# Half-piece runs, earlier table loads, reordered norm sums and unread products in a two-layer gated-mixer transformer kernel

## What is computed

```python
for l in range(DEPTH):
    ux = rmsnorm(h, g_pre_mix[l]) * (1 + sc1x) + sh1x
    yx, yc = token_mixers(ux, uc, ...)        # four attention branches A to D, gated, w_out
    h = h + ga1x * rmsnorm(yx, g_post_mix[l])
    ux = rmsnorm(h, g_pre_ffn[l]) * (1 + sc2x) + sh2x
    h = h + ga2x * rmsnorm(swiglu(ux, w_ffn_in[l], w_ffn_out[l]), g_post_ffn[l])
```

## Time and profile before

| | |
|---|---|
| median of 3 runs | 1987.03 us (1986.37 to 1988.64) |
| the profiled execution | 1986.53 us |
| its span, first to last instruction | 1984.1 us (2.4 us lie around it) |
| mean granted clock of TensorE | 0.962 of full speed |
| PE, DVE, ACT, POOL busy | 1832.9, 1218.5, 883.5, 679.9 us |

### The profile page before, as it was taken

One profiled execution on the slowest core, in us unless ns is written; L12 is line 12 of the kernel. 1 busy time (PEld: TensorE's weight loads), 2 busy tenths in 40 slices (PEclk: granted clock), 3 DMA queues, 4 the chain that ended last, 5 costly groups with the idle time before them and its releaser, 6 DMA issues. The chain is left out here.

```text
span 1984.1 us, 31794 instructions
## 1 busy us (share of the span) xinstructions
PE 1832.9 (92%) x10675; PEld 1584.5 (80%) x10675; DVE 1218.5 (61%) x2381; ACT 883.5 (45%) x1918; POOL 679.9 (34%) x615
## 2 busy tenths in 40 slices
PE   7888899999998999989999999788998889989998
PEld 7767778877877778778888878667887778879997
DVE  7345467776756865567677674655654446776654
ACT  2455544444433444452232333465554445555553
POOL 6143434445434544611111023134344444351100
PEclk9998999999998999979999999899999999989998
DMA  7221223333432323335456663123443333446663
GB/s 294 64 51 32 70 76 96 100 112 111 114 96 70 83 67 107 96 91 149 138 156 200 200 179 98 45 58 73 102 104 87 98 80 102 123 118 175 182 185 118
DMA packets 381802, 223.14 MB, mean 112 GB/s; under 512 B 51606, under 2 KB 377548, under 8 KB 380620
## 3 DMA queue, kind: packets, MB, share of 16 engines
q1 hardware_dynamic: 379340, 217.97, 38.8%
q10 hardware_dynamic: 2304, 3.15, 0.5%
HBM read 217.92 MB, written 3.15 MB: 111 GB/s over the span
## 5 line engine op out<-in xcount | busy, mean ns | idle before, releaser
L1808 PE MATMUL bank<-Uhi,w_ring 128*128 128x512 f32 (+2 forms) x1664 | 595.5, 358 | 27.9 <-DVE Ulo L1668 17.8
L1810 PE MATMUL bank<-Uhi,w_ring 128*128 128x512 f32 (+2 forms) x1664 | 580.5, 349 | 0.0
L1809 PE MATMUL bank<-Ulo,w_ring 128*128 128x512 f32 (+2 forms) x1664 | 580.0, 349 | 0.0
L1538 DVE TENSOR_TENSOR w_ring<-load_ring,w_ring 128x512 fp32r<-128x512 f32 (+2 forms) x432 | 337.6, 799 | 166.8 <-ACT w_ring L1353 140.9
L1353 ACT ACTIVATE w_ring<-load_ring 128x512 fp32r<-128x512 f32 (+4 forms) x640 | 368.6, 602 | 93.0 <-PE bank L1810 71.9
L1808 PEld LDWEIGHTS bank<-Uhi,w_ring 128*128 128x128 f32 (+1 forms) x1664 | 320.8, 193 | 74.7 <-issue 24.3
L1810 PEld LDWEIGHTS bank<-Uhi,w_ring 128*128 128x128 f32 (+1 forms) x1664 | 320.7, 193 | 40.8 <-issue 0.2
L1313 POOL TENSOR_TENSOR w_ring<-load_ring,w_ring 128x512 fp32r<-128x512 f32 (+3 forms) x208 | 248.0, 1195 | 297.5 <-ACT w_ring L1353 151.2
L1809 PEld LDWEIGHTS bank<-Ulo,w_ring 128*128 128x128 f32 (+1 forms) x1664 | 321.4, 193 | 35.1
L1808 PE MATMUL bank<-Z,w_ring 128*128 128x512 f32 (+2 forms) x784 | 272.8, 348 | 11.4 <-DVE Z L1783 5.9
L1810 PE MATMUL bank<-Z,w_ring 128*128 128x512 f32 (+2 forms) x784 | 268.6, 343 | 0.0
(11 more groups left out here) (138 smaller groups left out, 2403.5 us busy)
## 6 DMA issues: line engine op xcount, KB each, us to landing
load_ring<-in_w_in SPq DMA_DIRECT2D x192, 256.0 KB, 3.0
load_ring<-in_w_ffn_in SPq DMA_DIRECT2D x160, 256.0 KB, 3.1
mod_ring<-in_w_mod SPq DMA_DIRECT2D x96, 256.0 KB, 3.0
load_ring<-in_w_ffn_out SPq DMA_DIRECT2D x80, 256.0 KB, 3.3
mod_place<-in_w_mod SPq DMA_DIRECT2D x64, 256.0 KB, 2.8
load_ring<-in_w_branch SPq DMA_DIRECT2D x64, 256.0 KB, 2.9
mod_w<-in_w_mod SPq DMA_DIRECT2D x8, 1024.0 KB, 13.9
load_ring<-in_w_in SPq DMA_DIRECT2D x64, 128.0 KB, 2.6
```

Of the source, the lines that this page charges most:

```text
L1538: dve.tensor_tensor(w_ring[:, slot, 1, 0:sz], load_ring[:, plan.slot['load', key], 0:sz], w_ring[:, slot, 0, 0:sz].bitcast(F32), ALU.subtr ...
L1808: pe.matmul(dst, lhs[0], rhs[0], start=start, stop=False)
L1809: pe.matmul(dst, lhs[0], rhs[1], start=False, stop=False)
L1810: return pe.matmul(dst, lhs[1], rhs[0], start=False, stop=stop)
```

## The change

The kernel's plan changes in these places, and a few instructions with it.

1. A piece's run in the attention stages is two steps of two row tiles, `mm_a` and `mm_b`, in place of one; other steps and the other stream may stand between them. The places of the projection's steps within a unit's slots are a table for each branch (`SET_PLACES`).
2. The load of a bias table is a step of its own, two slots ahead of `bias`.
3. The running sum of `hz` is made by DVE (L1708 of the changed kernel) where POOL made it. The last square of y is taken ahead of `yev`, PE sums `ysq` first and the other two behind it in `sums_rest` (left out below), and `moment` has four DVE instructions in place of five.
4. A step `warm` on PE: 4 or 6 matmuls 128x512 of two constant tiles into a bank that nobody reads, behind the broadcasts of a turnover and twice at the end (38 in all).
5. In a turnover `apB` and `gmm` of a tile stand ahead of the residual steps of the tile three further on; a group's splits are emitted behind its `gmm` and counted one further.

```diff
 MOD_RATE = (0.2, 0.8, 1.6, 0.9)
 MOD_COST = {'modw': (0, 0.96, 1.93), 'modsum': (0, 0.3, 0.3)}
 MOD_US = 1.2
+
+
+SET_PLACES = {('A', 9): (0, 0, 0, .34, .34, .34, .4, .7, .7), ('B', 7): (0, .1, .2, .35, .35, .6, .7),
+              ('D', 9): (0, .1, .2, .3, .3, .45, .55, .75, .8),
+              ('D', 24): (0, 0, 0, 0, 0, .17, .17, .17, .17, .17, .17, .34, .34, .34, .34, .51, .51, .51, .51, .51, .68, .68, .84,
+                          .84)}
 AT_START = (3, 4)
 AHEAD = 4
...
+def halved(steps):
+
+
+    return [(kind, key, {}) for _, key, _ in steps for kind in ('mm_a', 'mm_b')]
+
+
 def win_pieces(l, name, c0, cols=P, halves=None):
 
...
-                p.take('fil', ('ap', nm, kt), ('ap_lo', (nm, kt)))
-                p.step('apA', (nm, kt), l=l, which=which, n=n)
-                for step in posts.get(kt, ()):
-                    step()
-            if kt:
-                p.step('apB', (nm, kt - 1), n=n)
-                p.step('gmm', (first, kt - 1))
+        def scaled(kt):
+            p.take('tmp', ('ap', nm, kt), ('ap_full', (nm, kt)))
+            p.take('fil', ('ap', nm, kt), ('ap_lo', (nm, kt)))
+            p.step('apA', (nm, kt), l=l, which=which, n=n)
+
+        scaled(0)
+        for step in posts.get(0, ()):
+            step()
+        for kt in range(KT):
+            if kt + 1 < KT:
+                scaled(kt + 1)
+            p.step('apB', (nm, kt), n=n)
+            p.step('gmm', (first, kt))
+            for step in posts.get(kt + 1, ()):
+                step()
 
     def post(nm, kt, n):
         p.step('post', (nm, kt), n=n)
...
 
-        p.step('sums', nmo, n=n, what=('ysq', 'hz', 'zsq'))
+        p.step('sums', nmo, n=n)
         p.step('sums_rest', nmo, n=n, what=('hz', 'zsq'))
         p.step('mstat', nmo, nh=1, dim=D, n=n, after=('first_sums', nmo))
         p.step('wide', nmo, n=n, of=1)
         p.take('bc', ('bc', nmo), ('post_scaled', (nmo, KT - 1)))
         p.step('bcast', nmo, n=n)
+        p.step('warm', nmo, times=4)
         p.step('moment', nm, n=n)
         p.step('pow', nm, n=n)
         p.step('wide', nm, n=n, of=4)
         p.take('bc', ('bc', nm), ('ap_scaled', (nm, KT - 1)))
         p.step('bcast', nm, n=n)
+        p.step('warm', nm, times=6)
         post(nmo, 0, n)
         post(nmo, 1, n)
...
                 vs = v_chain(key, gen, vfree, DH)
-                return [qs[0], (piece_cost(NTOK, 1), kv), qs[1], vs[0], (0, kstore), qs[2], vs[1], qs[3], vs[2]]
+                return [*qs[:3], (piece_cost(NTOK, 1), kv), vs[0], (0, kstore), qs[3], vs[1], qs[4], vs[2]]
             low = b.lower()
             halves = [j, j + 4] if b in 'BD' else None
             own = j * P if b == 'C' else 0
...
-            v0, v1, v_raw, v_turn, v_store = vs
-            return [k0, k1, k_raw, q0, k_sum, q1, q_raw, k_norm, v0, v1, v_raw, q_sum, k_rot, q_norm, k_store, v_turn,
-                    q_rot, q_store, v_store]
+                return ks[:5] + qs[:4] + [ks[5], qs[4]] + vs[:5] + [qs[5], ks[6], vs[5], qs[6], vs[6]]
+            k_raw, k_sum, k_norm, k_rot, k_store = ks[4:]
+            q_raw, q_sum, q_norm, q_rot, q_store = qs[4:]
+            v_raw, v_turn, v_store = vs[4:]
+            return ks[:4] + [k_raw, *qs[:2], k_sum, *qs[2:4], q_raw, k_norm, q_sum] + vs[:4] \
+                + [v_raw, q_norm, k_rot, k_store, v_turn, q_rot, q_store, v_store]
 
         def bias_steps(u, i):
 
             if i == 0:
...
+            p.step('bias', (u, i), l=l)
+
+        def table(u, i):
             p.take('tab', (u, i), ('bias_full', (u, i)))
             p.step('tab', (u, i))
-            p.step('bias', (u, i), l=l)
 
         def emit(item_no):
 
...
 
+            def half(self):
+
+
+                return bool(self.todo) and self.open
+
             def piece(self):
                 cost, make, _ = self.todo.pop(0)
                 make()
+                self.open = not self.open
                 self.flush()
                 while self.todo and not self.todo[0][0]:
                     self.late.append(self.todo.pop(0)[1])
@@ -611,11 +643,11 @@
                     c += 12 * SEQ if items[k - 2][2] == 'x' else 6 * SEQ
             return c
 
-        def spread_over(micro, slots):
+        def spread_over(micro, slots, of):
 
 
             whole, gone, out = sum(c for c, _ in micro), 0, [[] for _ in range(slots)]
-            places = {5: (0, .3, .3, .6, .7), 7: (0, .2, .2, .4, .55, .75, .8)}.get(len(micro))
+            places = SET_PLACES.get((of, len(micro)))
             for i, (c, make) in enumerate(micro):
                 at = places[i] * slots if places else (gone + c / 2) * (slots - .5) / whole
                 out[min(slots - 1, int(at))].append((c, make))
...
             while micro or fill.ready(owed):
-                more = fill.ready(owed)
+                more = fill.ready(owed) or fill.half()
                 if micro and (not micro[0][0] or not more or turn == 0):
                     cost, make = micro.pop(0)
...
                     kept[at_item + len(mine) - 1] = [micro.pop()[1]]
-                micros[at_item:at_item + len(mine)] = spread_over(micro, len(mine))
+                micros[at_item:at_item + len(mine)] = spread_over(micro, len(mine), u2[1])
                 if units[un + 1][0] == 'C':
                     for i in range(2):
                         bias_at[at_item + len(mine) - 2 + i] = (u2, i)
+                        table_at[at_item + len(mine) - 4 + i] = (u2, i)
             at_item += len(mine)
         forced = [base_cost(k) + sum(c for c, _ in micros[k]) for k in range(n_slots)]
         for n in range(4):
@@ -746,6 +783,8 @@
                     fill.todo += gate(dt, n) + (up(dt + 2, n - 1) if dt + 2 < KT else [])
             quota, owed = levels(forced[a:b], sum(c for c, _, _ in fill.todo)), 0
             for k in range(a, b):
+                if k in table_at:
+                    table(*table_at[k])
                 if k in bias_at:
                     bias_steps(*bias_at[k])
...
                     for g in range(3):
                         p.step('coef', (l + 1, g))
-                p.step('yev', key, n=nq, l=l, which=which)
+                if dt < KT - 1:
+                    p.step('yev', key, n=nq, l=l, which=which)
                 for what in whats:
                     if 0 < dt < KT - 1:
                         p.take('tmp' if what == 'hz' else 'fil', (what, key), (what[0] + '_added', key))
                     elif dt == KT - 1:
                         p.take('tmp' if what != 'ysq' else 'fil', (what, key), ('first_sums' if what == 'ysq' else 'sums_done', nmo))
                     p.step(what, key, n=nq)
+                    if dt == KT - 1 and what == 'ysq':
+                        p.step('yev', key, n=nq, l=l, which=which)
                 for what in whats if 0 < dt < KT - 1 else ():
                     p.step(what[0] + 'add', key, n=nq)
 
...
         p.take('w', key, ('piece_used', key))
-    order, done, first = [], 0, 0
+    order, done, first, used = [], 0, 0, set()
     for st in S:
-        if st[0] in ('mm', 'gmm', 'mstat'):
-            while done < min(len(use), first + AHEAD):
+        if st[0] == 'gmm':
+            order.append(st)
+            first += 1
+        if st[0] in ('mm', 'mm_a', 'gmm', 'mstat'):
+            while done < min(len(use), first + AHEAD - (st[0] == 'gmm')) and (
+                    done <= first or done < W_RING or use[done - W_RING] in used):
                 order.append(('split', use[done], {'raises': (p.lo[use[done]],)}))
                 done += 1
-            first += st[0] != 'mstat'
-        order.append(st)
+            first += st[0] in ('mm', 'mm_a')
+        if st[0] != 'gmm':
+            order.append(st)
+        if 'piece_used' in SIGNALS[st[0]]:
+            used.add(st[1])
     p.steps = order
 
     at = {(kind, key): i for i, (kind, key, _) in enumerate(order)}
...
                     dve.wait_ge(sem['sums_done'], count['sums_done', before])
-                    done = count['moment_part', key] - 4
+                    done = count['moment_part', key] - 3
                     r, a, h2 = stat[:, 1, 0:m], stat[:, 2, 0:m], stat[:, 5, 0:m]
                     dve.tensor_tensor(a, bank[5][:, 4:4 + m], r, ALU.mult).then_inc(sem['moment_part'], 1)
                     dve.wait_ge(sem['moment_part'], done + 1)
                     dve.scalar_tensor_tensor(out=a, in0=bank[5][:, 0:m], scalar=2.0, in1=a, op0=ALU.mult,
                                              op1=ALU.add).then_inc(sem['moment_part'], 1)
                     dve.wait_ge(sem['moment_part'], done + 2)
-                    dve.tensor_tensor(a, a, r, ALU.mult).then_inc(sem['moment_part'], 1)
+                    dve.scalar_tensor_tensor(out=a, in0=a, scalar=1.0 / D, in1=r, op0=ALU.mult,
+                                             op1=ALU.mult).then_inc(sem['moment_part'], 1)
                     dve.wait_ge(sem['moment_part'], done + 3)
```

(18 more changed lines are left out.)

114 lines of the change are left out of this document (68 added, 46 removed).

## The result

The changed kernel takes 1971.39 us (median of 4, 1968.15 to 1972.67) against 1987.23 for the kernel before on the same chip: ratio 0.9917, 95% interval 0.9900 to 0.9934, some 16 us faster. The forecast was 1936, its range 1912 to 1970: the sign was right, the gain a third of what the sum gave.

What follows compares the result with a forecast made beforehand. PE was taken as the bound, with holes: 151.2 us idle and about 75 us of clock cost. 1986.5 - 25 - 17 - 10 - 3 - 8.5 + 13 = 1936 us, range 1912 to 1970.

Steps and rivals of the forecast that it cites:

- Bias tables, -25: Branch C, both layers: loads two slots ahead end waits for tables and most of v's evacuation waits; 25 us less.
- Branch A of layer 0, -17: Layer 0's branch A: 60% of 18.3 us idle and 9.7 us clock cost goes; 17 us less.
- These four waits go: Layer 0's branch A: PE's 8.2 us in 4 waits for q's evacuation ahead of the rotary product vanish.
- The other 10 us there: Layer 0's branch A: remaining idle time, at stores of q and normalised scores right behind the rotary product; 10 us.
- rival 1: Waits re-form in A and D while tables and turnovers give what they should; 1960 us, chance 0.17.
- Turnovers, -8.5: Three turnovers and the end: earlier group products, full-rate clock, POOL's sums no longer last; 8.5 us less.
- the clock's 2.4 + 1.5 us: First two turnovers: PE kept working between broadcasts runs groups at full rate; 2.4 us, then 1.5 us less.
- Branch D, -10: Into D of layer 0: waits for q's store and widened roots shrink; layer 1 set at nothing; 10 us less.
- Branch A of layer 1, -3: Layer 1's branch A: only q's evacuation leaves the chain to the product with v; 3 us less.
- What comes back, +13: Losses: late splits behind two open runs, 7 us, and removed waits meeting the slot's next link, 6; 13 us more.
- Rival 3: Exponentials queued sooner hold ACT's queue, 0.7 us for each of 83 slots, 58 us; 1994 us, chance 0.05.
- Rival 4: Waits go as counted but half-rate stretches stay, so the clock's 23 us are not won; 1959 us, chance 0.05.

Runs made afterwards that it cites:

- experiment 6: Kernel before plus early tables, half runs and their orders in layer 0 alone, q's store ahead of v's transposes in layer 0's branch A; 1926.99 us, 0.9718.
- experiment 14: experiment 6 with the exponential in layer 0 placed behind 3200 columns of further work in place of 1000; 1921.54 us, 0.9682.
- experiment 2: Kernel before plus early bias tables and all that the change does at turnovers and output stages, pieces whole; 1971.18 us, 0.9948.
- 1: Kernel before with one edit, each bias table's load issued two slots earlier; 1961.80 us, 0.9898.
- 7: Changed kernel with the order within a turnover's group as before (residual pairs ahead of `apB`, splits ahead of the products); 1964.43 us, 0.9903.
- 9: experiment 6 plus the change's turnovers with the group's order of before (unread products, order of sums, `hz` on DVE kept); 1929.76 us, 0.9730.
- experiment 12: Changed kernel with the group's order of before, and in layer 1's branch D the square's evacuation and sum in different slots again; 1959.36 us, 0.9875.
- experiment 15: Kernel before plus early tables, q's store early in branch A of both layers, the change's order for D's first unit in layer 0, whole pieces; 1945.18 us, 0.9799.
- experiment 18: experiment 12 with gate and up-projection pieces whole in layer 1, and evacuations there following their half run before the exponential; 1944.75 us, 0.9816.
- 13: experiment 12 with the exponential in layer 1 placed behind 1600 columns of further work in place of 1000; 1958.09 us, 0.9864.
- 8: Changed kernel without the unread `warm` products; 1968.40 us, 0.9929.

## Why the prediction was wrong

**Bias tables, -25: right, -21.** The mechanism held: no wait for a table is left, and the edit alone gives 21 us. In layer 1 it gave 18.7. In layer 0 it gave 2.6, because three of the four waits of the earlier trace rows (5.0 us with tables alone) were not the tables', though I had booked them to them. They were not mainly the short distance between v's last product and its transposes either, 0.4 us before: with half runs, and by the prediction's count 2.8 us of PE work in between, they still are 4.0 to 4.1 us (after, experiment 6). They went when the exponential was put later (experiment 14).

**Branch A of layer 0, -17: the first step that failed; measured +1.** "These four waits go" was right. "The other 10 us there ... the new order has at least 3.2 us of PE work between them" was not: I measured the store's distance from the scores in PE work and not in what stands ahead of the store on ACT. There it was an exponential that waits for DVE. The wait moved one link on, from the rotary product to the scores (8.2 us gone, 7.4 more there), which is what rival 1 said of this stage. One swap took 13.9 us off it, so 17 was about what the place holds.

**Turnovers, -8.5: the second; measured +9 (experiment 2 against 1; 10.3 - 2.2 = 8.1 by the table's stages).** In the first turnover the second broadcast came 1.2 us later, for 1.1, the first product 1.0 us earlier, for 0.4, and the group ran at full rate. What failed is "the splits of the group have not moved, so nothing for them": they had moved, ahead of the residual pair on DVE, and each then waits for its high part on ACT. And the clock's 2.4 + 1.5 us were counted as time, where PE only waits longer for DVE. For the third turnover and the end I had 4 us; from D's last maximum to the end after is 0.3 us shorter than before. Some 4 us of the loss are shown to be the order's (experiments 7, 9, 12); the rest stays open, with the reordered sums as the untested suspect.

**Branch D, -10: right in layer 0 and more, wrong in layer 1.** 7.1 in D and, by experiment 15, 12.4 at the end of C, where D's first unit is projected, come of its new order. In layer 1 I named the loss (squares summed 0.7 us after their product) and "set these equal" with the store; it cost 7.3 (experiment 12). A unit has four slots there and six in layer 0, and the same table of fractions falls into other slots.

**Branch A of layer 1, -3: +2.6.** It comes with the half runs, as idle time (13.9 to 16.8 us); a later exponential takes 2.0 of that off.

**What comes back, +13: the size was right by luck, 12 in A to C of layer 1, the cause was not.** I had splits and next links; experiment 18 shows the exponential ahead of evacuations for 4.5 of it, and 13 for 2.0 in A, which D lost again. The tanh waits are open.

**The rivals.** The nearest is rival 1, the waits re-form: its 1960 holds 8.5 us of gain in the turnovers, and with their loss of 8 in its place it is 1976. Rival 3, the exponential holds ACT, I gave 0.05 for 58 us; it is real, at 5 to 7 us in layer 0 (experiment 14 against 6) and 4.5 in B and C of layer 1 (18, by stages), and it is behind the failure in A as well. It was thought of as one more delay for each of 83 slots; it decides only where the step queued behind the exponential is one that PE waits for next. Rival 4 is settled by experiments 8 and 9: in the turnovers the clock gives nothing, as PE is not what they wait for. In the mixers it comes with the holes: where A lost 9.3 us of idle time it lost 4.6 more.

The clock by itself: the loss by the mean granted clock was 3.8% of the span before and is 2.3% after, but the 75 - 45 = 30 us that this is worth on paper are not in the time: 13.4 us of PE are unread products, and in the turnovers PE waits at either rate. The Trainium skill (TensorE: Matmul & The Clock Gate, Part 1) puts the ramp's cost under 1% of a typical kernel's span. The prediction set that against the 3.8%, and it is not the same thing: 3.8% is the loss of all stretches at half rate, nearly all of them later in the span, while up to the first maximum, the first 119.7 us, the granted clock is 0.99, which is under 2 us. For the start the trace agrees with the page.

Early tables, the order of D's first unit and half runs in layer 0, q's store ahead of v's transposes, and a later exponential make 1921.54 us, 0.9682: 63 us under the 1984 us of the kernel before that ran beside it, more than this forecast's 51.

## What to carry to other kernels

When a wait is removed from a chain, ask of each later step which instruction stands ahead of it on its own engine, and what that one waits for; distance in the bound engine's work says nothing of that. A step that PE needs next goes ahead of one that waits for another engine, and a filler that has its operands goes into the wait, not behind it. A table of fractions must be read in slots for every number of slots that it is used with. And busy work that raises the clock pays only where the engine it speeds up is the one waited for.

## What the hardware showed that was not expected

An engine at the head of whose queue one instruction waits shows as idle for 2.67 us (exponential) or 1.81 us (split) with work right behind it, at a mean load of 45% and 63%: load says nothing of such waits. And 38 matmuls whose product nobody reads lift the mean granted clock from 0.972 to 0.977 and start a group at full rate, for 7.0 us more of busy PE, and leave the time within 3 us (1971.39 and 1968.40; by the ratios 2.4 us the other way).
